# The last pair of experts in a new order, and half copies of the chosen expert's weights

## The reference

```python
def hier_moe(u, wg_r, bg_r, we_r, be_r, w_gate, w_up, w_down):
    ...
    for e in range(N_EXPERTS):        # 16 experts, top 2 for each token
        h = jax.nn.silu(t @ w_gate[e]) * (t @ w_up[e])
        out = out + combine[:, e:e + 1] * (h @ w_down[e])
```

## Time and profile before

| | us |
|---|---|
| median of three runs | 1663.35 (1662.29 to 1663.72) |
| the profiled execution | 1663.33 |
| its span | 1661.4 |
| TensorE busy in the span | 1589.0 (96%) |
| VectorE busy | 830.7 (50%) |
| ScalarE busy | 735.7 (44%) |
| read from HBM | 285.05 MB |

### The profile page before, as it was taken

One profiled execution on the slowest core, in us unless ns is written; L12 is line 12 of the kernel. 1 busy time (PEld: TensorE's weight loads), 2 busy tenths in 40 slices (PEclk: granted clock), 3 DMA queues, 4 the chain that ended last, 5 costly groups with the idle time before them and its releaser, 6 DMA issues.

```text
span 1661.4 us, 26843 instructions
## 1 busy us (share of the span) xinstructions
PE 1589.0 (96%) x11188; PEld 1228.5 (74%) x11188; DVE 830.7 (50%) x1461; ACT 735.7 (44%) x1140; POOL 0.9 (0%) x5
## 2 busy tenths in 40 slices
PE   7999989999999999999989899999999989999987
PEld 5646667777787778689768899988988778535543
DVE  2536664634334344642676666655777765312223
ACT  3444552633213332542464644546545533455443
POOL 0000000000000000000000000000000000000000
PEclk9999999999999999999999999999999989999999
DMA  9412623254424433423112446453433227799995
GB/s 390 151 39 102 207 99 111 97 198 152 140 102 174 181 121 103 170 76 128 51 50 78 152 148 216 151 172 126 154 127 102 82 98 304 307 403 420 421 420 208
DMA packets 43132, 287.89 MB, mean 173 GB/s; under 512 B 4848, under 2 KB 6000, under 8 KB 12160
## 3 DMA queue, kind: packets, MB, share of 16 engines
q1 hardware_dynamic: 42832, 285.99, 45.9%
q10 hardware_dynamic: 144, 0.06, 0.0%
q0 software_dynamic: 32, 0.07, 0.0%
HBM read 285.05 MB, written 1.05 MB: 172 GB/s over the span
## 4 chain that ended last, share of the span: by engine, by line
PE 80%; DVE 9%; ACT 5%; DMA 4%; issue 2%; DVEq 0%; SPq 0%; ACTq 0%
PE ps L539 17%; PE ps L540 16%; PE ps L541 16%; PE ps L2952 7%; DMA deep<-wts 4%; DVE WL L524 2%; PE ps L584 2%; PE ps L2812 1%; PE ps L1553 1%; PE ps L1524 1%; PE ps L1455 1%; PE ps L564 1%; PE ps L702 1%; PE ps L1631 1%; PE ps L1632 1%
## 5 line engine op out<-in xcount | busy, mean ns | idle before, releaser
L539 PE MATMUL ps<-HH,WH 128*128 128x512 f32 (+2 forms) x1488 | 495.3, 333 | 22.4 <-DVE WL L524 11.0
L541 PE MATMUL ps<-HH,WL 128*128 128x512 f32 (+2 forms) x1488 | 483.9, 325 | 0.0
L540 PE MATMUL ps<-HL,WH 128*128 128x512 f32 (+2 forms) x1488 | 483.5, 325 | 0.0
L524 DVE TENSOR_TENSOR WL<-ring,WH 128x2048 fp32r<-128x2048 f32 (+2 forms) x134 | 281.7, 2105 | 146.0 <-ACT WH L514 146.0
L539 PEld LDWEIGHTS ps<-HH,WH 128*128 128x128 f32 x1488 | 284.4, 191 | 72.9 <-issue 33.4
L541 PEld LDWEIGHTS ps<-HH,WL 128*128 128x128 f32 x1488 | 284.5, 191 | 21.8
L514 ACT ACTIVATE WH<-ring 128x2048 fp32r<-128x2048 f32 (+2 forms) x134 | 235.8, 1762 | 144.0 <-PE ps L541 75.1
L540 PEld LDWEIGHTS ps<-HL,WH 128*128 128x128 f32 x1488 | 284.9, 191 | 19.5
L2952 PE MATMUL ps<-deep,arena 128*32 128x512 f32 (+1 forms) x872 | 114.3, 593 | 10.4 <-ACT late_x L2938 5.5
L539 PE MATMUL ps<-parts,WH 128*128 128x512 f32 (+1 forms) x352 | 119.7, 340 | 0.0
L540 PE MATMUL ps<-parts,WH 128*128 128x512 f32 (+1 forms) x352 | 118.4, 336 | 0.0
(11 more groups left out here) (400 smaller groups left out, 2105.4 us busy)
## 6 DMA issues: line engine op xcount, KB each, us to landing
ring<-wts SPq DMA_DIRECT2D x138, 1024.0 KB, 5.0
deep<-wts SPq DMA_DIRECT2D x92, 1024.0 KB, 16.4
ring<-wts SPq DMA_DIRECT2D x32, 704.0 KB, 4.1
arena<-wts SPq DMA_DIRECT2D x8, 1024.0 KB, 16.3
ring<-wts SPq DMA_DIRECT2D x4, 672.0 KB, 13.8
X<-xin SPq DMA_DIRECT2D x4, 512.0 KB, 17.2
ahead<-wts SPq DMA_DIRECT2D x2, 1024.0 KB, 8.7
deep<-wts SPq DMA_DIRECT2D x4, 512.0 KB, 20.5
```

The source lines that it names most:

```text
L524: e.tensor_tensor(lo, raw(i), hi.bitcast(F32), ALU.subtract).then_inc(*up("low", i))
L539: e.matmul(o, w[0][:, cols], x[0], start=k == 0, stop=False)
L540: e.matmul(o, w[0][:, cols], x[1], start=False, stop=False)
L541: return e.matmul(o, w[1][:, cols], x[0], start=False, stop=k == nk - 1)
```

## The change

The transfers of up 7 go ahead of those of down 6. TensorE does up 7, the first half of down 6, turn 7, the second half of down 6, the first half of down 7, scatter 6, the conditional block, the second half of down 7, scatter 7. Turn 7 is copied to a tile of its own, `HTL`, and needn't wait for down 6. ScalarE's copies go in the same order, and each copy, not only the last, is two instructions of 1024 columns, for each of which TensorE waits by itself. On ScalarE the conditional block stands between y 6 and the copies of down 7's second step. The conditional block's own waits (PE, ACT, DVE, SP) are for the end of down 6 in place of down 7 where they waited for the latter.

```diff
@@ chunk_plan
+        if e == NP - 1:
+            p += [(("eu", x, i), 2048) for i in range(2) for x in (e, partner(e))]
         if e:
             p += [(("ed", x, i), 2048) for i in range(2) for x in (e - 1, partner(e - 1))]
-        if e < NP:
+        if e < NP - 1:
             p += [(("eu", x, i), 2048) for i in range(2) for x in (e, partner(e))]
...
+        HTL = arena[:, 12864:13376]
@@ act_other
-            if (kind, p, i) == LAST:
...
-            e.wait_ge(*chunks_landed(q))
+            last = (kind, p, i) == LAST
+            if not last:
+                e.wait_ge(*chunks_landed(q))
             if q >= 2:
                 e.wait_ge(*at("used.pair", q - 2))
-            e.activation(OTHER[q % 2], m[:, bass.ds(v + a, SLOT)], ACT.Copy).then_inc(*up("other", q))
+            for n in range(2):
+                if last:
+                    e.wait_ge(s_last[n], 32)
+                e.activation(OTHER[q % 2][:, 1024 * n:1024 * n + 1024], m[:, bass.ds(v + a + 1024 * n, 1024)],
+                             ACT.Copy).then_inc(*up("other", q, n))
@@ pe_pair_in
-                e.wait_ge(*at("other", q))
                 for k in range(4 * i, 4 * i + 4):
+                    if k % 2 == 0:
+                        e.wait_ge(*at("other", q, k // 2 % 2))
@@ pe_pair_out
-                e.wait_ge(*at("other", q))
...
-                    e.wait_ge(*at("other", q, n))
+                e.wait_ge(*at("other", q, n))
                 for k in (2 * i, 2 * i + 1):
...
+                    h = HTL if p == NP - 1 else HT2
@@ pe_experts
+                if p == NP - 1:
+                    break
                 if p:
                     pe_pair_out(e, p - 1, 0)
                     pe_pair_out(e, p - 1, 1)
                 pe_pair_in(e, "eu", p)
-                if p + 1 < NP:
-                    pe_side(e, p + 1)
+                pe_side(e, p + 1)
+            flag_load(e, "pe")
+            pe_pair_in(e, "eu", NP - 1)
+            pe_pair_out(e, NP - 2, 0)
             pe_pair_turn(e, NP - 1)
-            flag_load(e, "pe")
+            pe_pair_out(e, NP - 2, 1)
+            pe_pair_out(e, NP - 1, 0)
             pe_scatter(e, NP - 2)
-            pe_pair_out(e, NP - 1, 0)
-            pe_pair_out(e, NP - 1, 1)
             with over_capacity(e, "pe"):
                 pe_over(e)
+            pe_pair_out(e, NP - 1, 1)
             pe_scatter(e, NP - 1)
@@ act_experts
-            for p in range(NP):
+            for p in range(NP - 1):
...
+            act_other(e, "eu", NP - 1, 0)
+            act_silu(e, NP - 1)
+            act_other(e, "eu", NP - 1, 1)
+            act_other(e, "ed", NP - 2, 0)
+            act_other(e, "ed", NP - 2, 1)
             flag_load(e, "act")
             act_other(e, "ed", NP - 1, 0)
-            act_other(e, "ed", NP - 1, 1)
+            act_y(e, NP - 2)
             with over_capacity(e, "act"):
                 act_over(e)
+            act_other(e, "ed", NP - 1, 1)
             act_y(e, NP - 1)
@@ dve_pair_turn
+            if p == NP - 1:
+                e.tensor_copy(HTL, B("expert_turn", p)).then_inc(*up("ht", p))
+                return
@@ dve_experts
+                if p == NP - 1:
+                    break
                 if p:
                     dve_y(e, p - 1)
                 dve_up(e, p)
+            dve_up(e, NP - 1)
             flag_load(e, "dve")
             dve_pair_turn(e, NP - 1)
+            dve_y(e, NP - 2)
             dve_scatter(e, NP - 2)
```

## The result

| | before | changed |
|---|---|---|
| median, us | 1664.28 (16 runs, 1662.29 to 1666.21) | 1667.68 (16 runs, 1663.48 to 1669.61) |
| ratio, with its 95% interval | | 1.0016 (1.0009 to 1.0023) |
| profiled execution, span | 1663.33, 1661.4 | 1669.38, 1667.5 |

The change makes the kernel slower: by the ratio 2.7 us, by the medians 3.4. The forecast was +0.1 us.

The account below looks back on a forecast made before the run. The prediction took the last stage as bound by weight transfers, with 6.6 us of TensorE work behind them. Transfers 0, down 7 ending at 1647.23 instead of 1647.11 and an unchanged 14.3 us tail gave 1663.4 us, range 1661.4 to 1664.8.

Parts of the forecast that it names:

- What bounds the kernel: From 1460 us on the last stage is bound by weight transfers at 420 or 421 GB/s; 6.6 us of work follow the stream.
- part 1: Order of the transfers, up 7 ahead of down 6: nothing comes earlier or later, 0 us.
- Part 2: Half copies: TensorE can start 0.86 us earlier behind an arrival; ScalarE pays at most 0.2 us more.
- Part 3: End of the last pair in the new order: from the 1635.45 arrival, scatter 6 ends at 1642.27, down 7 at 1647.23.
- Part 4, the branch: Jump over the experts past capacity: its price of 1.21 us moves ahead of the second half of down 7.
- The clock: TensorE's clock, at 1.00 (2.4 GHz) in all the rows read from the stage, was held to be no part of the argument.
- The tail: From the end of down 7 to the end of the span: 14.3 us, said to stay in either order.
- The sum: End of down 7 at 1647.23 in place of 1647.11, +0.1 us, so 1663.4 us in all.
- the likeliest rival: The branch costs little where it stands now, or the 1.21 us had another cause: -1.2 us, 1662.1; chance 0.22.
- the 108 ns: Price of a compare and branch by the Trainium skill; with it the sum was said to give 1662.2, a small gain.
- The slower rival: ScalarE's jump delays the last chunk's copies (1664.1), or TensorE's additional waits ahead of 1460 shift the stream (1664.6); chance 0.15.
- The range: For 8 in 10, 1661.4 to 1664.8 us: the sum, branch covered and slower cases, with the spread of the runs.

## Why the prediction was wrong, step by step

- **What bounds the kernel, and part 1.** Right. The stream runs at 417 to 421 GB/s in the same stretches, and the last chain starts at the same distance from the first gather, within 0.05 us.
- **Part 2.** Right. The half copies alone brought 0.82 us (0.86 forecast) and cost nothing ahead of 1460: with them the last copy starts 225.56 us behind the first gather, 225.65 without.
- **Part 3 up to scatter 6.** Right within 0.2 us (227.55 against 227.36): the first half of down 7 took 3.64, not 3.50, and the scatter 2.23, not 2.12.
- **Part 4, the branch.** Here it failed. The step was: "I take the 1.21 us as the price of the jump." That was the part of the jump that could be seen. The whole, from the first instruction packet to the next matmul, is 2.4 to 3.1 us, and 1.8 of it lay beneath the long matmuls queued ahead of it. The row that said so was open to view: the packet of the instruction queue came before the matmuls had ended, not behind them. The prediction rested on the one microsecond of the earlier trace rows and gave the q14 packet there to the jump; the q8 packet at 1645.3 is 1.2 us older. The argument against the rival, that "the matmuls before it didn't cover it either", fails at the same point. Moved behind scatter 6, the jump lost its cover: 2.75 in place of 1.21, +1.54 us.
- **The clock.** A term that the sum left at nothing: "it is no part of the argument" was said of the rows before, where the longest rest was 1.2 us. Behind 2.75 us the clock fell to 1.2 GHz, and the matmuls took 5.37 in place of 3.75: +1.62 us.
- **The tail.** It gained 0.39 us (13.90 in place of 14.29 from the end of down 7 to the end of the span), where none was forecast. ScalarE's squares start 2.04 us behind down 7's end (1655.64 - 1653.60), not 2.21, and take 2.65 in place of 2.87, as VectorE's adds are further ahead (the first starts 1.26 us behind down 7's end, 1654.86 - 1653.60, where it was 1.73). The prediction had this add end at 2.1 "in either case".
- **The sum.** 0.12 forecast, 0.19 up to scatter 6, 1.54, 1.62, less 0.39: 3.08. The profiles give 249.57 - 246.49 = 3.08.
- **The rivals.** That the branch costs little where it stands was the likeliest rival, and wrong in sign. (By its own terms it gives 1662.2 and the 108 ns 1662.3, each 0.1 more than written.) The slower rival had the right kind of cause (a jump that takes longer than 1.21) on the wrong engine: ScalarE's own jump delayed nothing. The Trainium skill, "Runtime: NRT & Kernel Launch", section Instruction fetch mechanics, speaks of a fetch of the target's page on a taken branch, and the trace agrees: a 16 KB packet of q8 at each jump of TensorE, and none there in the version without a block. That the q14 packet belongs to the jump, as the prediction drew from it, no run bears out. The 108 ns of the Trainium skill, "Advanced Engine Details and Errata", section Control Flow Timing, are at odds with the rows: no jump here took less than 2.4 us from packet to matmul.
- **The range.** 1661.4 to 1664.8 was built around 1.21 as if this were a measured price. Bounds of 0 and, say, the distance from the q8 packet (3.0 us) would have reached 1665.2 and opened the question of the clock, though even then, without the clock's 1.6 us, the range would have ended below the measured 1667.68. Also the base of 1663.35 was the median of three runs; of 16 it is 1664.28.

Left open: why the sequencer doesn't go ahead of the scatter. That its matmuls are of fewer columns isn't enough, since 16 of them take 2.23 us, more than the 1.8 us of cover. They wait for banks that VectorE frees, which may hold the sequencer back; no run took these waits away. Also why one of five profiles kept its clock, behind a rest of 2.78 us when another fell behind 2.07.

## What to carry to other kernels

A jump's visible rest is what is left of it after its cover: look for the packet of the instruction queue ahead of the rest, and count from there before moving the jump. Here its rest was short, and mostly off the path, behind long queued matmuls and beside a stretch where other engines hold the path; it was longest beside a full stream. A rest of 2 to 3 us on TensorE cost up to 1.7 us more behind it, through the clock.

## What the runs showed of the hardware

- A taken jump on TensorE: 2.4 to 3.1 us from the first instruction packet (16 KB) to the next matmul, in the ten profiles of the table.
- The same jump, with the queues at 411 GB/s (one profile of each): the packet started 2.5 us later against the matmuls' end (-0.7 in place of +1.8) than at 12 GB/s. The Trainium skill, "DMA: Bandwidth & Descriptors", section Queues, rings and completion order, says that an engine drains a whole packet from one ring before it turns to the next; that would make an instruction fetch wait its turn behind weights. No run here shows the turns themselves.
- TensorE's clock: behind rests of 2.07, 2.75, 2.82, 3.11 and 3.62 us it fell to 0.50 for part of the next matmuls, behind one of 2.78 it didn't; behind the rests of 0.67 to 1.21 at a jump it stayed at 1.00 for the matmuls that came next (32 long ones in 3.67 us in the kernel before with its block moved). Each of these falls made 32 matmuls take 5.34 to 5.37 in place of 3.64 to 3.75 us.
